# One memory stage instead of two in a fused two-block kernel on one Trainium2 core

## The reference, cut to what matters

```
def peer_ffn(xn, w_q, keys1, keys2, u_tab, v_tab):      # xn: 512 x 1024, tables: 16384 x 1024
    q = (xt @ w_q).reshape(T, 8, 2, 64)
    s1 = einsum('thd,kd->thk', q[:, :, 0], keys1)        # 128 keys each
    s2 = einsum('thd,kd->thk', q[:, :, 1], keys2)
    v1, i1 = top_k(s1, 16); v2, i2 = top_k(s2, 16)
    cand = (v1[..., :, None] + v2[..., None, :]).reshape(T, 8, 256)
    cidx = (i1[..., :, None] * 128 + i2[..., None, :]).reshape(T, 8, 256)
    top, pos = top_k(cand, 16);  eidx = take_along_axis(cidx, pos)
    g = softmax(top)
    a = gelu(einsum('td,thkd->thk', xc, u_tab[eidx]))    # 128 picked rows of u per token
    return einsum('thk,thkd->td', g * a, v_tab[eidx])    # the same rows of v
```

## Time and profile before

| | |
|---|---|
| median of 3 runs | 3219.04 us |
| profiled execution, own time | 3222.66 us |
| its span in the trace | 3220.8 us |
| busy: TensorE / VectorE / GpSimd / ScalarE | 86% / 46% / 23% / 15% |
| bytes moved by DMA | 693.93 MB |

### The profile page before, as it was taken

The page is one execution under the profiler, slowest core; times in us unless marked ns, Lnnn a source line. Parts: engine busy times, 40 slices in busy tenths (PEclk is TensorE's granted clock), DMA queues, the critical chain, the costliest instruction groups (busy, mean ns, idle before and its releaser), DMA issues. The chain is left out here.

```text
span 3220.8 us, 30219 instructions
## 1 busy us (share of the span) xinstructions
PE 2779.2 (86%) x10080; PEld 1558.2 (48%) x10080; DVE 1478.4 (46%) x3007; ACT 489.8 (15%) x1015; POOL 732.9 (23%) x652
## 2 busy tenths in 40 slices
PE   6997899999997599959889989998980678888877
PEld 3445534447443433314435578887870543333333
DVE  1226200104012222232047249888679977777762
ACT  2124100001101011131137121111110310000002
POOL 0000000000000022110000004554466046766740
PEclk8997998999999699979999999999995999999998
DMA  5100251340122699941300019999999069999992
GB/s 203 50 27 28 105 192 43 134 173 37 52 79 83 268 392 396 387 187 60 111 14 1 27 60 346 413 399 354 418 415 365 38 248 413 413 414 413 413 363 85
DMA packets 133341, 693.93 MB, mean 215 GB/s; under 512 B 19571, under 2 KB 20979, under 8 KB 105587
## 3 DMA queue, kind: packets, MB, share of 16 engines
q1 hardware_dynamic: 50644, 408.32, 32.0%
q0 software_dynamic: 81792, 281.07, 22.1%
q10 hardware_dynamic: 800, 3.15, 0.3%
HBM read 701.90 MB, written 48.23 MB: 233 GB/s over the span
## 5 line engine op out<-in xcount | busy, mean ns | idle before, releaser
L428 PE MATMUL ps<-hT,wring 128*128 128x256 f32 (+1 forms) x2576 | 763.0, 458 | 30.2 <-ACT pk_g L2250 14.9
L428 PEld LDWEIGHTS ps<-hT,wring 128*128 128x128 f32 x2576 | 491.3, 191 | 296.7 <-issue 252.7
L2469 PE MATMUL ps<-pm_v_rows,pm_weighted 128*128 128x512 f32 x1024 | 465.2, 604 | 62.6 <-DVE pm_weighted L2519 44.7
L2144 POOL DMA_INDIRECT pk_ring<-in_peer_u,pk_rows x256 | 304.0, 1187 | 765.3 <-DVEq L2358 538.9
L2286 DVE CUSTOM_DVE_ANT_0 pk_ring<-pk_ring,mem_x 128x1024 f32<-128x1024 f32 x256 | 309.3, 1223 | 100.6 <-DMA pk_ring<-in_peer_u,pk_rows 87.9
L2469 PEld LDWEIGHTS ps<-pm_v_rows,pm_weighted 128*128 128x128 f32 x1024 | 186.6, 190 | 340.5 <-issue 230.4
L2437 POOL DMA_INDIRECT hT<-in_peer_v,pm_idxs x192 | 258.4, 1346 | 206.3 <-PE ps L2457 107.8
L2525 DVE SCALAR_TENSOR_TENSOR h_tok<-hT,gates,h_tok 128x1024 f32<-128x1024 f32 x192 | 244.7, 1282 | 100.4 <-DMA hT<-in_peer_v,pm_idxs 81.9
L1417 POOL COPY ex_idx<-row_token 128x1 uint32 (+1 forms) x24 | 4.4, 183 | 1222.3 <-PEq L1549 1090.3
L960 PE MATMUL ps<-wring,hT 128*128 128x512 f32 (+1 forms) x544 | 213.9, 555 | 1.2 <-PEq L376 1.2
L1604 DVE TENSOR_SCALAR hT<-ps,gain,ada 128x128 f32<-128x128 f32 x192 | 63.4, 403 | 215.9 <-PE ps L1505 215.9
(11 more groups left out here) (422 smaller groups left out, 2943.9 us busy)
## 6 DMA issues: line engine op xcount, KB each, us to landing
ex_gu<-in_experts SPq DMA_DIRECT2D x32, 2048.0 KB
pm_v_rows<-in_peer_v SPq DMA_DIRECT2D x64, 1024.0 KB
ex_dn<-in_experts SPq DMA_DIRECT2D x48, 1024.0 KB
wring<-in_w_in SPq DMA_DIRECT2D x21, 2048.0 KB, 8.9
wring<-in_peer_uT SPq DMA_DIRECT2D x21, 2048.0 KB
wring<-in_experts SPq DMA_DIRECT2D x16, 2048.0 KB
ada_w<-in_w_ada SPq DMA_DIRECT2D x12, 2048.0 KB
pk_u<-in_peer_uT SPq DMA_DIRECT2D x11, 2048.0 KB
```

Source lines behind the costliest of these rows:

```text
L428: mm = env.nc.tensor.matmul(out, w[:, k, lo:hi], rhs(k), start=(k == 0), stop=(k == KD - 1))
L2144: nc.gpsimd.indirect_dma_start(ring[:, n % RING, :], None, dram["peer_u"], bass.IndirectOffsetOnAxis(ap=rows[:, n // SLOTS, n % SLOTS:n % ...
L2469: mm = nc.tensor.matmul(env.ps[:, OUT[n], :], W[q][:, j * DS + t * P:j * DS + (t + 1) * P], vr[j // 2][:, j % 2 * D + half * WBLK:j % 2 * ...
```

## The change

The two stages become one, `stage_memory`, with one set of SBUF buffers. C lies over the buffers of the ranking (they are free once all picks are known) and, from group 19 on, over the buffers of the score blocks. The steps in the order of the diff:

- u comes in pairs of blocks (1 MB) into four buffers of its own (UBUF = 4), gelu values leave in pairs from four buffers (GBUF = 4), as rows of 2 KB into halves of the rows of `g_dram`; before, rows of 4 KB.
- TensorE waits for `gate_s` = 4 behind block 83 (TABLE[3] = 84). Then follow 19 times (EARLY): one group of C, and its share of the remaining 44 blocks (`beside`). The other 13 groups come after block 127.
- ScalarE takes the exponentials of tile 3 behind block 83 instead of block 69.
- VectorE, when the ranking is over, makes one one-hot group and then a nineteenth of the dots that are left, 19 times; then 13 groups without dots between.
- One ring of 8 buffers, on the weight ring `wring`, serves the gathers of both tables: `n` runs from 0 to 511, and the first gathers of v are issued as soon as the last dots free their buffers. The index copies of the old loop (L2428) are gone.
- SP loads W for m = 0 to 3 behind group 18, but the rows of v (`vr`) and the second W only when the last group's product is done, since they lie where the one-hot matrices lay.
- The output loop is written out instead of `Fori`, and starts the sums with `start=(m == 0)` instead of a product with zeros.

```diff
-UBUF = 3
-TABLE = (8, 36, 66)
+UBUF = 4
+GBUF = 4
+TABLE = (8, 36, 66, 84)
+EARLY = 19
+def beside(n):
+    at = lambda k: TABLE[3] + (PK - TABLE[3]) * k // EARLY
+    return at(n), at(n + 1)
@@ gpsimd
-                for n in range(GT * SLOTS):
-                    if n % SLOTS == 0:
-                        pool.wait_ge(rows_s, n // SLOTS + 1)
+                for n in range(2 * GT * SLOTS):
+                    if n < GT * SLOTS:
+                        name, t, j = "peer_u", n // SLOTS, n % SLOTS
+                        if j == 0:
+                            pool.wait_ge(rows_s, t + 1)
+                    else:
+                        name, t, j = "peer_v", n % GT, n // GT - SLOTS
                     if n >= RING:
...
@@ sync
+                for t in c_t[EARLY - 1]:
+                    product_done(env, sp, t)
+                for n in range(QUADS):
+                    if n >= 2:
+                        sp.wait_ge(out_done, QUAD * (n - 1))
+                    nc.sync.dma_start(W[n % 2], dram["g_dram"][n]).then_inc(w_got[n % 2], 16)
+                    if n == 0:
+                        for t in c_t[-1]:
+                            product_done(env, sp, t)
+                    for m in (2 * n, 2 * n + 1):
+                        if m >= 2:
+                            sp.wait_ge(out_done, 2 * (m - 1))
+                        nc.sync.dma_start(vr[m % 2], v_pairs[m]).then_inc(v_got[m % 2], 16)
@@ tensor
-                table(TABLE[1], PK)
+                scores(TABLE[1], TABLE[3])
                 pe.wait_ge(gate_s, NT)
...
+                for n in range(GROUPS):
+                    coefficients(n)
+                    if n < EARLY:
+                        scores(*beside(n))
@@ scalar
-                table(TABLE[2], TABLE[2] + 4)
+                scores(TABLE[2], TABLE[3])
                 exponentials(3)
-                table(TABLE[2] + 4, PK)
...
@@ vector
+                def one_hot(n):
+                    A, B = one_hots(n)
+                    ts = slice(n * GRP, (n + 1) * GRP)
+                    if n in (0, 1):
+                        for tl in key_t:
+                            evacuated(env, ve, tl)
+                    elif n == EARLY:
+                        product_done(env, ve, u_t[-1])
+                    else:
+                        product_done(env, ve, c_t[n - 2][1])
+                    key = lambda k: keyT[:, k, ts].unsqueeze(2).broadcast_to(wide)
+                    V.tensor_tensor(B, iota[:].unsqueeze(1).broadcast_to(wide), key(1), ALU.is_equal).then_inc(ab_done, 1)
+                    V.tensor_tensor(A, iota[:].unsqueeze(1).broadcast_to(wide), key(0), ALU.is_equal).then_inc(ab_done, 1)
+                    ve.wait_ge(ab_done, 3 * n + 1)
+                    V.tensor_tensor(B, B, key(2), ALU.mult).then_inc(ab_done, 1)
...
                 finish(NT - 1)
-                for _ in range(GT * SLOTS):
-                    dot()
+                done = dot() + 1
+                for n in range(EARLY):
+                    one_hot(n)
+                    upto = done + (GT * SLOTS - done) * (n + 1) // EARLY
+                    while done < upto:
+                        done = dot() + 1
+                for n in range(EARLY, GROUPS):
+                    one_hot(n)
```

More of the change, by code:

```diff
@@ new lines, in stage_memory @@
+    u_t += env.tiles(TABLE[3] - TABLE[1])
+    key_t, c_t = env.tiles(2), []
+    for n in range(GROUPS):
+        c_t.append(env.tiles(2))
+        if n < EARLY:
+            u_t += env.tiles(beside(n)[1] - beside(n)[0])
+    turns = list(env.turns)
+    OUT = [0, 1, 2, 3]
+    blks = [env.take_block(q_t[1][3]), env.take_block(q_t[1][7])]
+    u_in, u0 = zip(*(env.again(f"table_in{n}", 16 * PAIRS // UBUF) for n in range(UBUF)))
+    (w_got, w0), (v_got, v0) = (zip(*(env.again(f"table_in{n}", c) for n in ns)) for ns, c in (
+        ((0, 1), 16 * QUADS // 2), ((2, 3), 16 * PAIRS // 2)))
@@ new lines, in stage_memory @@
+    got, got0 = zip(*(env.again(f"gathered{r}", 16 * 2 * GT * SLOTS // RING) for r in range(RING)))
+    g_out = [env.sem(f"pm_g_out{n}") for n in range(GBUF)]
+    in_s, top_s, exp_s, rows_s, gate_s = (env.sem("pm_" + n) for n in ("in", "top", "exp", "rows", "gate"))
+    used, ab_done, act_s, coef_s, w_done, out_done, sum_s = (env.sem("pm_" + n) for n in (
+        "used", "onehot", "gelu", "coef", "weighted", "out", "sum"))
+    v_pairs = dram["peer_v"].rearrange("(a c b) d -> c a (b d)", c=PAIRS, b=2)
@@ new lines, in stage_memory, with one_hots @@
+    ring = [env.wring[:, r // 4, r % 4 * D:(r % 4 + 1) * D] for r in range(RING)]
+    spare = env.hT[:].rearrange("p k t -> p (k t)")
+    vr = [spare[:, n * 2 * D:(n + 1) * 2 * D] for n in range(2)]
+    W = [spare[:, (4 + n) * D:(5 + n) * D] for n in range(2)]
+    def one_hots(n):
+        if n < EARLY:
+            return [env.hT[:, :, lo + n % 2 * P:lo + (n % 2 + 1) * P] for lo in (S, 0)]
+        return [spare[:, (lo + n % 2) * D:(lo + n % 2 + 1) * D].rearrange("p (t a) -> p t a", a=PK) for lo in (0, 2)]
@@ L2167, in _ @@
                         store(n - UBUF)
[L2168 removed]
+                for n in range(PAIRS - UBUF, PAIRS):
                     store(n)
[L2170 to L2171 removed]
+                for n in range(GBUF):
+                    sp.wait_ge(g_out[n], 16 * PAIRS // GBUF)
+                for t in c_t[EARLY - 1]:
[11 more added lines that the diff above has]
+                        nc.sync.dma_start(vr[m % 2], v_pairs[m]).then_inc(v_got[m % 2], 16)
             @block.tensor
@@ L2360, in _ @@
                     else:
-                        group(ve, [V.tensor_copy(pairs[:, t - GT], pick[:])])
+                        group(ve, [V.tensor_copy(pairs[:, t - GT], pick)])
                     if t >= 1:
@@ new lines, in _ @@
+                for tl in c_t[-1]:
+                    evacuated(env, ve, tl)
+                for m in range(PK):
+                    n = m // QUAD
+                    if m % QUAD == 0:
+                        ve.wait_ge(w_got[n % 2], w0[n % 2] + 16 * (n // 2 + 1))
+                    here = W[n % 2][:, m % QUAD * DS:(m % QUAD + 1) * DS]
+                    V.tensor_tensor(here, here, C[:, :, m], ALU.mult).then_inc(w_done, 1)
+                    for t in range(GT):
+                        k = GT * SLOTS + GT * m + t
+                        r = k % RING
+                        ve.wait_ge(got[r], got0[r] + 16 * (k // RING) + 16)
+                        ve.wait_ge(used, k - 1)
+                        V.scalar_tensor_tensor(env.h[:, t, :], ring[r], coef[:, t, m:m + 1], env.h[:, t, :],
+                                               ALU.mult, ALU.add).then_inc(used, 1)
@@ L2679, in second_block @@
     stage_norm(env, "ffn2", tok, [(0, NT, gain("g_ffn"), None)], env.hT)
-    G = env.picked
-    G.used = env.sem("mem_used")
-    G.got, G.got0 = zip(*(env.again(f"gathered{r}", 16 * 2 * GT * SLOTS // RING) for r in range(RING)))
-    with nc.sbuf_tensor("mem_x", [P, GT, D], F32) as xg:
-        stage_memory_scores(env, xg, G)
-    env.close_ring()
-    stage_memory_outputs(env, G)
-    env.open_ring()
+    stage_memory(env)
     stage_norm(env, "ple", tok, [(0, NT, gain("g_ple"), None)], env.hT)
```

365 lines of the change are left out of this document (134 added, 231 removed).

## The result

The change made the kernel slower. Medians: 3250.93 us after (3246.99 to 3259.67, 4 runs), 3217.06 before (3214.98 to 3221.66, 4 runs), ratio 1.0107, 95% interval 1.0083 to 1.0131. The forecast was 3168, range 3152 to 3194. The profiled execution took 3251.27 us, its span is 3249.4.

A forecast was written before the change was run, and what follows sets the result against it. Memory stages were taken as bound by DMA bytes, except a hole of some 110 us set by VectorE. Terms -67.7 + 17 + 0 = -51 us gave 3172 for the profiled execution, 3168 for the median, range 3155 to 3189, reaching 3152 to 3194.

The forecast's parts named there:

- Part 2: From the ranking's end to the last dot: last dot ends at 2506 against 2488.95, later by 17 us.
- Does TensorE let it?: Behind the ranking: TensorE's 19 groups and 44 score blocks take 191 us, done at 2480, before VectorE.
- Does GpSimd?: Behind the ranking: one gather per 1.05 + 0.30 us on GpSimd, so 110 take 152 of 216 us, covered.
- Rival B: Behind the ranking: one-hot operations slow GpSimd's gathers, VectorE's idle time is not recovered; net -4 us, 3215; chance 0.10.
- The wait for rows: Dots behind the ranking: VectorE idles 5 us for DMA, ends 0 and 20.
- End of ranking: Ranking's end: 2283 instead of 2294.9, with gathers alone beside it for some 45 us; ends 2276.7 and 2299.
- Part 1: Hole between last dot and output loop: 13 groups stay, 48.0 us instead of 115.7, shorter by 67.7 us.
- Part 4: Output loop: bound by the same bytes, first products some 5 us after the slice; cost 0, ends 0 and 5.
- Part 3: Score blocks: smaller u buffers cost 0; 2 KB gelu rows cost 3.5 us of DMA, 1.2 behind the ranking.
- The exponentials: Score blocks from 69 on: with tile 3's exponentials behind block 83, TensorE's stall of 14.9 us goes.
- Rival A: Dots behind the ranking keep their earlier pace beside block traffic, 2.0 us each; net +39 us, 3258; chance 0.07.
- Rival C: Behind the ranking: TensorE's clock stays at 1.2 GHz after some 50 us of rest; result above 3330; chance 0.03.

## Why the prediction was wrong

**The step that failed** is in Part 2, "Does TensorE let it?": "Per group 10.05 us against 11.36". It rests on what the step ahead of it assumed, "each group has its 2 or 3 blocks and 6 or 7 dots". Both sums are right as sums (TensorE 191 us, VectorE 215.8), but two engines that hand over to each other in every group take about the sum over the groups of the longer part, not the longer sum. With the shares as written, the dots' cost per group runs from 3.4 + 17 x 1.28 = 25 us down to 3.4, against 8.7 to 12.15 on TensorE all through. An estimate with the table above, with 3.41 us for a group's matrices, 1.145 for each dot (their pitch on end, shown below), and 8.7 or 12.15 for TensorE: the longer parts add up to 256 us, and with VectorE's 40.3 us of waits for rows that is 296 of the 305.6 measured from the ranking's end to group 19. Group 19 was forecast for 2506 and came at 2586. Even shares, which the step assumed, were built: 3179.47. That is 71.5 of the 82.9 us between forecast and result.

**The second mis-sized term** is "Does GpSimd?": 1.05 + 0.30 us per gather, "covered". In the changed kernel a gather takes 1.474 us, with even shares 1.571: 110 x 1.87 = 206 us, against 118 x 1.145 + 64.8 = 200 us of VectorE's own work, so no longer covered. Rows 7 stood for it, and there VectorE was far from idle (35.55 of 38 us in 2402 to 2440), but each dot came a little late, at a pitch of 1.28 us, the same as that of the gathers. The two engines of the kernel before, and VectorE's dots on end after the change:

```profile
2403.02 0.98 POOL L2144 DMA_INDIRECT pk_ring<-in_peer_u,pk_rows  x1 [0.30 <-issue]
2404.31 0.95 POOL L2144 DMA_INDIRECT pk_ring<-in_peer_u,pk_rows  x1 [0.30 <-issue]
...
2403.22 1.22 DVE L2286 CUSTOM_DVE_ANT_0 pk_ring<-pk_ring,mem_x 128x1024 f32<-128x1024 f32 x1
2404.52 1.23 DVE L2286 CUSTOM_DVE_ANT_0 pk_ring<-pk_ring,mem_x 128x1024 f32<-128x1024 f32 x1
```
```profile
2330.47 1.22 DVE L2388 CUSTOM_DVE_ANT_0 wring<-wring,pm_coef_table 128x1024 f32<-128x1024 f32 x1
2331.62 1.22 DVE L2388 CUSTOM_DVE_ANT_0 wring<-wring,pm_coef_table 128x1024 f32<-128x1024 f32 x1
```

So a gap of 0.02 to 0.06 us in front of each dot goes with an issue of 0.95 to 0.99 us (2402 to 2411), and no gap with 1.99. Rival B had the mechanism, but put it on the one-hot operations; the dots do it too, once they run on end. The price of the two-input form by run is 17 us with even shares, which is more than the 11.5 by which even shares missed the forecast (14 and 7 by the ratios); without it they are 6 us under it.

**Two terms that offset.** The 1.28 us of a dot was that same pitch, of dots that each wait a little; one whose row is there follows in 1.145, which makes 118 of them 16 us shorter. The wait for rows was put at 5 us and is 23.4 with even shares. So the 222.8 us of the forecast from the ranking's end to the last dot came out at 225.8 by luck; the rest of the miss of group 19 (2519.05 for 2506) is the ranking's end, 6.5 us later than forecast, and 3.8 us between the last dot and block 127's end. One step of the range is reckoned wrong besides: 3194 lies a fifth of the way from 3189 to B's 3215, not a third.

**What held.** End of ranking 2280.5 (forecast 2283; by the same code it was 2278.9 and 2289.5 in other executions, so the closeness is in part luck), and TensorE stands 51.6 us before it (50). Part 1: from group 19 to m = 0, 2633.97 - 2586.10 = 47.9 us (48.0). Part 4: first products 4.3 us after the slice (5), the stretch behind m = 0 unchanged, 413 GB/s. Part 3: 2 KB rows cost nothing that can be told, and TensorE has no wait for a block of u from 2000 on after the change; what the smaller buffers cost by themselves was not measured. The exponentials: stall gone. Rival A's pace (2.0 us per dot) did not come beside the blocks with even shares: 118 dots and 19 groups took 2515.3 - 2289.5 = 225.8 us, of which groups 64.8, so 1.36 per dot. Rival C: the clock was granted at 0.68 in the window with TensorE's long waits, where a group's products took 3.78 us instead of 2.05, and at 1.00, 2.4 GHz, once it worked on end; it did not stay at 1.2 GHz.

Roughly right in the forecast was the worth of the idea; wrong was that this code carries it out. That even shares and a wait at block 92 give the forecast's own time, 3168.69, is luck: a later wait and slower gathers, neither of them in the forecast, offset each other.

## What to carry to other kernels

Where two engines hand over per group, work out each group's share on both, from the loop's own formula with two or three values put in, and compare group by group; equal totals say nothing. Keep work that fills DMA spread over the work that doesn't. And take the duration of an issue on GpSimd from a stretch in which VectorE does what it will do after the change: busy to 94% with tiny gaps is not the same as busy on end.

## What the runs showed of the hardware

- An indirect gather of 128 rows takes GpSimd 0.94 us to issue, but 1.98 to 1.99 beside VectorE instructions with two SBUF inputs and a 128x1024 output that follow each other without a gap; with a one-input sum of the same length it stays at 0.94 (1.474 against 1.031 us on average in the same kernel). With 0.02 to 0.06 us between the two-input instructions it took 0.95 to 0.99. Whether the input or the output does it stays open.
- Storing rows of 2 KB instead of 4 KB costs nothing that can be told (ratio 0.9995).
- The end of the ranking, by the same code, moved by 11 us between profiled executions (2278.9, 2280.5 and 2289.5).
